# First token tile of a mixture-of-experts sum: weighted on TensorE by diagonal products, with the order of the tile's steps changed

## The chip, the cores and the metric

One core of a Trainium2 chip runs the whole program. The metric is device time in microseconds (us), the median of several executions.

## What is computed

Two transformer blocks for 512 tokens of width 1024. The first has differential attention, a state-space branch and a mixture of 32 experts, of which each token takes four; the second has a recurrent branch and dilated attention. The change lies where the first block ends and the second begins:

```python
y_rows = y_rows * row_gate[:, None]
y = jnp.zeros((n_tok, d)).at[row_tok].add(y_rows)     # four expert rows per token, each with its gate
x = x + g2[:, None, :] * y
x = _rmsnorm(x, final_g)
h = rms_norm(x, g_norm) * (1.0 + scale[:, None, :]) + shift[:, None, :]
q, k, v, ... = split(h @ w_in)
```

## The kernel before

The experts have written their output rows to `y_rows` in memory, one row per token and choice. The 512 tokens are four tiles (0 to 3) of 128. After the last expert the four tiles pass through the same steps, tile after tile, each engine in the fixed order in which its program is written; semaphores are all that joins the engines.

- **GpSimd** (`gpsimd_engine`, L2467) issues 16 indirect gathers, four per tile: 128 rows of 1024 floats each into `parts`. Tile 0's four have a semaphore each ("first parts k gathered"), the other tiles one for all four.
- **VectorE** (`vector_engine`): `add_part(t, k)` (L2168, L2170) multiplies a tile's gathered rows by their gates and adds them up, in four instructions of 128x1024. `residual(t)` (L2181, eight of 128x128, in two halves of four) adds the turned sum times `g2` to `x_t`. `tile_scale(t)` (L2187) is one reciprocal; `tile_scaled(t)` (L2193, eight of 128x128) makes `h_t` from `x_t`.
- **TensorE** (`tensor_engine`): `second_bias(t)` (L1037) puts the gated output bias in the two banks of tile t's sum. `turn_sum(t)` (L1045) transposes the sum of VectorE onto it, eight products of 128 columns with the identity. `norm_sums(t)` (L1053) makes sums over the squares, eight products of 2 columns. `spread_scale(t)` (L1059) puts the scale on all partitions. `v_rows(t, i)` (L1071) is the first real work of block two: half i of the value projection, eight products of 512 columns. `keep_on(count, bank)` (L610) issues `count` products of 512 columns whose result nobody reads ("idle products" below).
- **ScalarE** (`scalar_engine`): `tile_squares(t)` (L1519, two halves), `tile_root(t)` (L1523), `tile_shifted(t)` (L1528, eight pieces, each releasing one product of `v_rows`), `keep_v_rows(t, i)` (L1532). After tile 0's shift it issues the load of two tables (positions and the recurrent gates).
- **SyncE** loads the second half of the value weights once tile 0's fourth gather has landed, and waits for all gathers before it goes on to the weight pairs (L1112 are their products).

Every fp32 product is two passes on TensorE, so eight products are 16 records in the trace. The order on TensorE from the bias of tiles 0 to 2 on is: 6 idle products, `turn_sum(0)`, 2 idle, `norm_sums(0)`, 2 idle, `spread_scale(0)`, `turn_sum(1)`, `v_rows(0, 0)`, `norm_sums(1)`, `v_rows(0, 1)`, `spread_scale(1)`, `turn_sum(2)`, `v_rows(1, 0)`, and so on.

Of the kernel before, what the change touches and what calls it, by code (L numbers as in the profile page):

```python
# [14 lines left out]
P = 128  # L15
S = 512
D = 1024
KT = D // P
# [7 lines left out]
EXPERTS, TOPK = 32, 4  # L26
# [16 lines left out]
NP = len(PASSES)  # L43
# [74 lines left out]
def program(nc, io):  # L118


    with ExitStack() as ctx:
# [3 lines left out]
        def sem(name):  # L125
            if name not in sems:
                sems[name] = ctx.enter_context(nc.semaphore(name.replace(" ", "_")))
            return sems[name]
# [31 lines left out]
        psum = ctx.enter_context(nc.psum_tensor("psum", [P, 8, S], F32))  # L160
# [134 lines left out]
        pos_i = pos_i.bitcast(I32)  # L295
        parts = arena[:, 0:16 * D].rearrange("p (n d) -> p n d", n=16)
        g2 = mods[:, 40:48]
        rstd, rstd2 = work[:, 8, :], work[:, 8, :]
# [237 lines left out]
        def tensor_engine():  # L536
# [494 lines left out]
            def second_bias(t):  # L1031
# [7 lines left out]
                mm.then_inc(sem("bias in banks"), 1)  # L1039

            def turn_sum(t):
                a = SUM_AT[t]
                pe.wait_ge(sem("parts summed"), t + 1)
                for k in range(KT):
                    mm = pe.matmul(psum[:, a + k // 4, (k % 4) * P:(k % 4 + 1) * P], parts[:, t * TOPK, k * P:(k + 1) * P], identity, start=False, stop=True, skip_group_check=True)  # L1045
                    if k % 4 == 3:
                        mm.then_inc(sem("sum turned"), 1)
# [15 lines left out]

            def v_rows(t, i):
                if t == 0:
                    pe.wait_ge(sem(f"slot {4 + 4 * i} loaded"), 32 if i else V_LOADED)
                else:
                    pe.wait_ge(sem("v rows kept"), 2 * t + i - 1)
                for k in range(KT):
                    pe.wait_ge(sem("h ready"), 8 + KT * t + k + 1)  # L1070
                    mm = pe.matmul(psum[:, 4 + i, :], h_t[:, k, t * P:(t + 1) * P], ring[:, 4 * i + 4:4 * i + 8, k, :], start=(k == 0), stop=(k == KT - 1))  # L1071
                mm.then_inc(sem("v product"), 1)

# [5 lines left out]
            second_bias(2)  # L1079
            keep_on(6, 0)  # L1080
            turn_sum(0)
            keep_on(2, 0)
            norm_sums(0)
            keep_on(2, 0)
            spread_scale(0)
            turn_sum(1)
            v_rows(0, 0)
            norm_sums(1)
            v_rows(0, 1)
            spread_scale(1)  # L1090
# [149 lines left out]
        def scalar_engine():  # L1240
# [298 lines left out]
            act.dma_start(pos_i, io["positions"]).then_inc(sem("late tables loaded"), 16)  # L1539
            act.dma_start(arena[:, low:low + 2048], io["rnn_gates"]).then_inc(sem("late tables loaded"), 16)  # L1540
            tile_squares(1)
            keep_v_rows(0, 0)
            tile_root(1)
# [124 lines left out]
        def vector_engine():  # L1668
# [492 lines left out]
            def add_part(t, k):  # L2161
                acc = parts[:, t * TOPK, :]
                if t == 0:
                    dve.wait_ge(sem(f"first parts {k} gathered"), 16)
                elif k == 0:
                    dve.wait_ge(sem(f"parts {t} gathered"), 16 * TOPK)
# [22 lines left out]
            def tile_scaled(t):  # L2189
                dve.wait_ge(sem("scale spread"), t + 1)  # L2190
                dve.wait_ge(sem("moe added"), 2 * t + 2)
                for k in range(KT):
                    dve.scalar_tensor_tensor(h_t[:, k, t * P:(t + 1) * P], x_t[:, k, t * P:(t + 1) * P], gain2[:, k:k + 1], psum[:, 0, t * P:(t + 1) * P], ALU.mult, ALU.mult).then_inc(sem("h scaled"), 1)  # L2193

            for k in range(TOPK):
                add_part(0, k)
            residual(0)
            for k in range(3):
                add_part(1, k)
            tile_scale(0)  # L2200
            add_part(1, 3)
            tile_scaled(0)
            residual(1)
# [482 lines left out]
```

## Time and profile before

| | us |
|---|---|
| median of 3 runs | 1996.19 |
| lowest and highest | 1994.83, 1996.49 |
| the profiled execution, its own time | 1998.96 |
| its span, first to last instruction | 1997.7 |
| TensorE busy in the span | 1937.8 (97%) |
| VectorE busy | 836.2 (42%) |
| ScalarE busy | 424.7 (21%) |
| GpSimd busy | 240.0 (12%) |
| mean granted clock of TensorE | 0.987 |

Times in the trace count from the span's start. The stage of the change lies between 1340 and 1442 us. A granted clock of 1.00 is 2.4 GHz, one of 0.50 is 1.2 GHz. The difference between the profiled execution's own time and its span, 1.3 us, lies around the instructions.

### The profile page before, as it was taken

How to read it: one execution, taken by the hardware profiler on the slowest of the kernel's cores; microseconds unless marked ns; L12 is line 12 of the kernel's file. 1: busy time of each engine (PE TensorE's matmuls, PEld its weight loads, DVE VectorE, ACT ScalarE, POOL GpSimd, SP SyncE). 2: the span in 40 equal slices, each digit the busy share in tenths (PEclk: the TensorE clock that was granted, in tenths of full speed). 3: DMA queues.
4: the chain of work that ended last, by engine and by line, in shares of the span. 5: the costliest groups of instructions: out<-in, count | busy, mean ns of one | idle time of the engine just before them, and what ended most of it. 6: DMA issues, size and time to landing. Idle time of an engine off the chain costs nothing.

```text
span 1997.7 us, 38345 instructions
## 1 busy us (share of the span) xinstructions
PE 1937.8 (97%) x16481; PEld 1079.1 (54%) x16481; DVE 836.2 (42%) x1530; ACT 424.7 (21%) x914; POOL 240.0 (12%) x173
## 2 busy tenths in 40 slices
PE   8999998999999999999999999989999999999998
PEld 4455544433434434343443433345588888888887
DVE  5989875211121211121120211105458678654465
ACT  3223512210111110011010111102233443431102
POOL 0000000000000000000000000002244334360011
PEclk8999998999999999999999999998999999999999
DMA  8475796999799999999999999975112112122221
GB/s 339 139 282 195 286 335 268 420 419 366 319 421 419 420 420 419 421 419 420 419 419 420 418 420 416 419 295 225 63 68 89 67 67 89 66 85 85 85 85 64
DMA packets 103419, 553.94 MB, mean 277 GB/s; under 512 B 14224, under 2 KB 25488, under 8 KB 48336
## 3 DMA queue, kind: packets, MB, share of 16 engines
q1 hardware_dynamic: 81344, 516.84, 64.1%
q10 hardware_dynamic: 14848, 17.82, 2.7%
q0 software_dynamic: 7056, 16.79, 2.3%
q8 instruction: 133, 2.18, 0.4%
q14 instruction: 38, 0.31, 0.0%
HBM read 532.91 MB, written 26.35 MB: 280 GB/s over the span
## 4 chain that ended last, share of the span: by engine, by line
PE 72%; DMA 13%; SPq 10%; DVE 3%; issue 2%; ACT 1%; another core or an unknown queue 0%; ACTq 0%; DVEq 0%
PE psum L1112 24%; PE psum L926 19%; DMA arena<-in_w 9%; SPq L467 9%; PE psum L934 9%; PE psum L597 7%; PE psum L1071 3%; DMA ring<-in_w 2%; DMA arena<-in_mod_slabs 1%; PE psum L919 1%; PE psum L1199 1%; PE psum L1218 1%; PE psum L942 1%; PE psum L906 1%; PE psum L781 1%
## 5 line engine op out<-in xcount | busy, mean ns | idle before, releaser
L926 PE MATMUL psum<-arena,ring 128*32 128x512 f32 x4096 | 452.7, 596 | 11.3 <-DMA arena<-in_w 10.8
L926 PEld LDWEIGHTS psum<-arena,ring 128*32 128x32 f32 x4096 | 134.3, 110 | 310.1 <-issue 307.1
L2114 DVE TENSOR_SCALAR h_t<-psum 128x512 f32<-128x512 f32 (+2 forms) x33 | 27.9, 845 | 572.5 <-PE psum L926 572.5
L934 PE MATMUL psum<-arena,h_t 128*32 128x256 f32 x3840 | 217.9, 380 | 4.2 <-DMA arena<-in_w 3.3
L1458 ACT ACTIVATE ring<-psum,mods,gain 128x64 f32<-128x64 f32 (+2 forms) x264 | 85.6, 429 | 607.5 <-PE psum L906 607.5
L934 PEld LDWEIGHTS psum<-arena,h_t 128*32 128x32 f32 x3840 | 120.7, 110 | 101.1 <-issue 18.7
L2435 POOL DMA_INDIRECT ring<-h_rows,row_i x33 | 35.5, 1075 | 1144.0 <-PE psum L906 834.9
L1112 PE MATMUL psum<-ring 128*128 128x256 f32 x768 | 171.1, 379 | 0.0
L1112 PEld LDWEIGHTS psum<-ring 128*128 128x128 f32 x768 | 145.9, 190 | 20.1 <-issue 0.3
L1112 PE MATMUL psum<-h_t,ring 128*128 128x256 f32 x672 | 154.3, 379 | 0.2 <-ACT arena L1532 0.2
L926 PE MATMUL psum<-ring 128*32 128x512 f32 x1344 | 148.8, 593 | 5.5 <-DMA ring<-in_w 5.4
L1112 PEld LDWEIGHTS psum<-h_t,ring 128*128 128x128 f32 x672 | 126.4, 190 | 23.8 <-issue 7.7
L597 PE MATMUL psum<-h_t,ring 128*128 128x512 f32 x256 | 116.8, 611 | 2.5 <-ACT h_t L1278 2.5
L1112 PE MATMUL psum<-arena,ring 128*128 128x256 f32 x544 | 119.1, 379 | 0.0
L1112 PEld LDWEIGHTS psum<-arena,ring 128*128 128x128 f32 x544 | 103.3, 190 | 14.2 <-DVE arena L2268 0.2
L926 PEld LDWEIGHTS psum<-ring 128*32 128x32 f32 x1344 | 44.4, 110 | 103.4 <-issue 103.4
L934 PE MATMUL psum<-ring,h_t 128*32 128x256 f32 x1600 | 90.9, 380 | 3.8 <-DMA ring<-in_w 3.1
L2128 DVE COPY h_t<-psum 128x512 f32<-128x512 f32 (+2 forms) x33 | 27.9, 845 | 154.9 <-PE psum L942 154.9
L597 PEld LDWEIGHTS psum<-h_t,ring 128*128 128x128 f32 x256 | 48.7, 195 | 62.9 <-issue 61.8
L1466 ACT ACTIVATE work<-psum 128x512 f32<-128x512 f32 (+2 forms) x33 | 23.8, 720 | 240.8 <-PE psum L934 240.8
L934 PEld LDWEIGHTS psum<-ring,h_t 128*32 128x32 f32 x1600 | 50.2, 110 | 43.8 <-issue 7.8
L1112 PE MATMUL psum<-work,ring 128*128 128x256 f32 x256 | 60.7, 380 | 1.7 <-DVE work L2268 1.7
(480 smaller groups left out, 2132.6 us busy)
## 6 DMA issues: line engine op xcount, KB each, us to landing
arena<-in_w SPq DMA_DIRECT2D x288, 1024.0 KB, 30.9
ring<-in_w SPq DMA_DIRECT2D x96, 1024.0 KB
ring<-in_pairs SPq DMA_DIRECT2D x40, 1024.0 KB, 4.8
ring<-in_dot_slabs SPq DMA_DIRECT2D x40, 512.0 KB, 5.9
ring<-in_mod_slabs SPq DMA_DIRECT2D x6, 2048.0 KB, 9.2
ring<-in_proj_slabs SPq DMA_DIRECT2D x24, 512.0 KB, 4.4
y_rows<-arena SPq DMA_DIRECT2D x3, 3584.0 KB, 25.0
y_rows<-work ACTq DMA_DIRECT2D x70, 64.0 KB, 7.7
```

What stands on the lines that cost most here:

```text
L467: sp.dma_start(slot[s], source).then_inc(sem(f"weights {s} loaded"), 16)
L597: mm = pe.matmul(bank, ring[:, n % 4, k, :], src[:, k, :], start=(k == 0), stop=(k == KT - 1))
L781: mm = pe.matmul(bank, w_glu[:, m, k, :], proj[:, k, :], start=(k == 0), stop=(k == 3))
L926: mm = pe.matmul(psum[32 * j:32 * j + 32, g, :], x_e[:, c * tokens + g * TG:c * tokens + g * TG + TG], slot[s][:, j * S:(j + 1) * S], star ...
L934: mm = pe.matmul(psum[32 * j:32 * j + 32, 6 + g // 2, (g % 2) * 256:(g % 2) * 256 + 256], h_e[:, g * 256 + half * P + 32 * c:g * 256 + hal ...
L1071: mm = pe.matmul(psum[:, 4 + i, :], h_t[:, k, t * P:(t + 1) * P], ring[:, 4 * i + 4:4 * i + 8, k, :], start=(k == 0), stop=(k == KT - 1))
L1112: mm = pe.matmul(out, stationary[:, k, :], moving[:, k, :], start=(start and k == 0), stop=(k == 3), skip_group_check=True)
L1458: act.activation(x_e[:, k * tokens:(k + 1) * tokens], psum[:, 4 + k // 4, (k % 4) * tokens:(k % 4 + 1) * tokens], ACT.Identity, bias=mods[ ...
L1466: act.activation(dst[:, 0:256 * groups], src[:, 0:256 * groups], ACT.Copy).then_inc(sem("y kept"), 1)
L2114: dve.tensor_scalar(gate, psum[:, 0:groups, 0:256], LIMIT, None, ALU.min).then_inc(sem("gate clipped"), 1)
L2128: dve.tensor_copy(h_e[:, 0:256 * groups], src[:, 0:256 * groups]).then_inc(sem("h_e kept"), 1)
L2435: pool.indirect_dma_start(out=x_g[n][0:rows, :], out_offset=None, in_=h_rows, in_offset=bass.IndirectOffsetOnAxis(ap=index, axis=0), bound ...
```

## The change

Tile 0's weighted sum is no longer made on VectorE. VectorE makes four diagonal matrices (`by_gate`, the identity times one gate column each, 128x128), and TensorE multiplies each gathered part by its diagonal matrix, as soon as that part's semaphore allows, adding up in the same banks in which the bias lies (`turn_parts`). The transposition comes with it, so `turn_sum(0)` goes. The six idle products before it go too, and of the two behind `norm_sums(0)` one.

The order changes as well: `v_rows(0, 0)` now stands ahead of `turn_sum(1)`, and `norm_sums(1)` stands in the middle of `v_rows(0, 1)`. On VectorE all of tile 1's sum comes behind `tile_scaled(0)`. On ScalarE `keep_v_rows(0, 0)` comes ahead of `tile_squares(1)`.

```diff
--- before.py
+++ after.py
@@ -294,6 +294,7 @@
         halves = [tile(n)[0:ROT, :] for n in (7, 10)]
         pos_i = pos_i.bitcast(I32)
         parts = arena[:, 0:16 * D].rearrange("p (n d) -> p n d", n=16)
+        by_gate = x_g[1][:, 0:TOPK * P].rearrange("p (k n) -> p k n", k=TOPK)
         g2 = mods[:, 40:48]
         rstd, rstd2 = work[:, 8, :], work[:, 8, :]
         v_sb = arena[:, 0:4096].rearrange("p (h t n) -> p h t n", h=HEADS2, t=TT)
@@ -1038,9 +1039,19 @@
                                    start=(k % 4 == 0), stop=False, skip_group_check=True)
                 mm.then_inc(sem("bias in banks"), 1)
 
+            def turn_parts():
+                a = SUM_AT[0]
+                pe.wait_ge(sem("gates laid out"), TOPK)
+                for part in range(TOPK):
+                    pe.wait_ge(sem(f"first parts {part} gathered"), 16)
+                    for k in range(KT):
+                        mm = pe.matmul(psum[:, a + k // 4, (k % 4) * P:(k % 4 + 1) * P], parts[:, part, k * P:(k + 1) * P], by_gate[:, part, :], start=False, stop=(part == TOPK - 1), skip_group_check=True)
+                        if part == TOPK - 1 and k % 4 == 3:
+                            mm.then_inc(sem("sum turned"), 1)
+
             def turn_sum(t):
                 a = SUM_AT[t]
-                pe.wait_ge(sem("parts summed"), t + 1)
+                pe.wait_ge(sem("parts summed"), t)
                 for k in range(KT):
                     mm = pe.matmul(psum[:, a + k // 4, (k % 4) * P:(k % 4 + 1) * P], parts[:, t * TOPK, k * P:(k + 1) * P], identity, start=False, stop=True, skip_group_check=True)
                     if k % 4 == 3:
@@ -1061,7 +1072,7 @@
 
             V_LOADED = 16 * (1 + 2 * (ROWS_TO - 2) + 2 * (9 - ROWS_TO) + 1)
 
-            def v_rows(t, i):
+            def v_rows(t, i, between=None):
                 if t == 0:
                     pe.wait_ge(sem(f"slot {4 + 4 * i} loaded"), 32 if i else V_LOADED)
                 else:
@@ -1069,6 +1080,8 @@
                 for k in range(KT):
                     pe.wait_ge(sem("h ready"), 8 + KT * t + k + 1)
                     mm = pe.matmul(psum[:, 4 + i, :], h_t[:, k, t * P:(t + 1) * P], ring[:, 4 * i + 4:4 * i + 8, k, :], start=(k == 0), stop=(k == KT - 1))
+                    if between and k == 3:
+                        between()
                 mm.then_inc(sem("v product"), 1)
 
             pe.wait_ge(sem("b2 loaded"), 32)
@@ -1077,16 +1090,14 @@
             second_bias(0)
             second_bias(1)
             second_bias(2)
-            keep_on(6, 0)
-            turn_sum(0)
+            turn_parts()
             keep_on(2, 0)
             norm_sums(0)
-            keep_on(2, 0)
+            keep_on(1, 0)
             spread_scale(0)
+            v_rows(0, 0)
             turn_sum(1)
-            v_rows(0, 0)
-            norm_sums(1)
-            v_rows(0, 1)
+            v_rows(0, 1, lambda: norm_sums(1))
             spread_scale(1)
             turn_sum(2)
             v_rows(1, 0)
@@ -1538,8 +1549,8 @@
             act.sem_inc(sem("held"), 1)
             act.dma_start(pos_i, io["positions"]).then_inc(sem("late tables loaded"), 16)
             act.dma_start(arena[:, low:low + 2048], io["rnn_gates"]).then_inc(sem("late tables loaded"), 16)
+            keep_v_rows(0, 0)
             tile_squares(1)
-            keep_v_rows(0, 0)
             tile_root(1)
             keep_v_rows(0, 1)
             tile_shifted(1)
@@ -2160,9 +2171,7 @@
 
             def add_part(t, k):
                 acc = parts[:, t * TOPK, :]
-                if t == 0:
-                    dve.wait_ge(sem(f"first parts {k} gathered"), 16)
-                elif k == 0:
+                if k == 0:
                     dve.wait_ge(sem(f"parts {t} gathered"), 16 * TOPK)
                 if k == 0:
                     then(dve.tensor_scalar(acc, acc, gates[:, t, 0:1], None, ALU.mult))
@@ -2192,14 +2201,14 @@
                 for k in range(KT):
                     dve.scalar_tensor_tensor(h_t[:, k, t * P:(t + 1) * P], x_t[:, k, t * P:(t + 1) * P], gain2[:, k:k + 1], psum[:, 0, t * P:(t + 1) * P], ALU.mult, ALU.mult).then_inc(sem("h scaled"), 1)
 
+            dve.wait_ge(sem("x turned"), NP)
             for k in range(TOPK):
-                add_part(0, k)
+                dve.tensor_scalar(by_gate[:, k, :], identity, gates[:, 0, k:k + 1], None, ALU.mult).then_inc(sem("gates laid out"), 1)
             residual(0)
-            for k in range(3):
+            tile_scale(0)
+            tile_scaled(0)
+            for k in range(TOPK):
                 add_part(1, k)
-            tile_scale(0)
-            add_part(1, 3)
-            tile_scaled(0)
             residual(1)
             for k in range(TOPK):
                 add_part(2, k)
```

TensorE, from behind the bias products of tiles 0 to 2 to the first value products (L610 idle products, L1045 `turn_sum`, L1053 `norm_sums`, L1059 `spread_scale`, L1071 `v_rows`), before:

```order
L610 MATMUL psum<-consts 128x512 x6
L1045 MATMUL psum<-consts,arena 128x128 [waits parts_summed]
L1045 MATMUL psum<-consts,arena 128x128 x7
L610 MATMUL psum<-consts 128x512 x2
...
L610 MATMUL psum<-consts 128x512 x2
L1059 MATMUL psum<-consts,par 128x128 [waits tile_scale]
L1045 MATMUL psum<-consts,arena 128x128 [waits parts_summed]
L1045 MATMUL psum<-consts,arena 128x128 x7
L1071 MATMUL psum<-ring,h_t 128x512 [waits h_ready,slot_4_loaded]
L1071 MATMUL psum<-ring,h_t 128x512 [waits h_ready] x7
```

The same stretch in the changed kernel (L1048 `turn_parts`, L611 idle products, L1070 `spread_scale`, L1082 `v_rows`, L1056 `turn_sum`):

```order
L1048 MATMUL psum<-ring,arena 128x128 [waits first_parts_0_gathered,gates_laid_out]
L1048 MATMUL psum<-ring,arena 128x128 x7
...
L1048 MATMUL psum<-ring,arena 128x128 [waits first_parts_3_gathered]
L1048 MATMUL psum<-ring,arena 128x128 x7
L611 MATMUL psum<-consts 128x512 x2
...
L611 MATMUL psum<-consts 128x512
L1070 MATMUL psum<-consts,par 128x128 [waits tile_scale]
L1082 MATMUL psum<-ring,h_t 128x512 [waits h_ready,slot_4_loaded]
L1082 MATMUL psum<-ring,h_t 128x512 [waits h_ready] x7
L1056 MATMUL psum<-consts,arena 128x128 [waits parts_summed]
```

The products that carry tile 0's sum wait for the gathers themselves, and `v_rows(0, 0)` has moved ahead of tile 1's transposition.

VectorE in the changed kernel, from the end of the experts (L2206 the diagonal matrices, L2190 `residual`, L2196 `tile_scale`, L2202 `tile_scaled`, L2177 and L2179 `add_part`):

```order
L2206 TENSOR_SCALAR ring<-consts,cols 128x128 [waits x_turned]
L2206 TENSOR_SCALAR ring<-consts,cols 128x128 x3
L2190 SCALAR_TENSOR_TENSOR x_t<-psum,mods,x_t 128x128 [waits sum_turned]
...
L2196 RECIPROCAL par<-par 128x1 [waits tile_root]
L2202 SCALAR_TENSOR_TENSOR h_t<-x_t,par,psum 128x128 [waits moe_added,scale_spread]
L2202 SCALAR_TENSOR_TENSOR h_t<-x_t,par,psum 128x128 x7
L2177 TENSOR_SCALAR arena<-arena,cols 128x1024 [waits parts_1_gathered]
L2179 SCALAR_TENSOR_TENSOR arena<-arena,cols 128x1024 [waits dve_order] x3
```

Tile 1's first three `add_part` stood ahead of the reciprocal, and its fourth between the reciprocal and `tile_scaled(0)`; all four now follow `tile_scaled(0)`.

## Rows read from the trace of the kernel before

**Rows 1.** The page: the span.
```profile
span 1997.7 us, 38345 instructions
```

**Rows 2.** The chain of waits, 1330 to 1450 us: start, us, what.
```profile
1369.27 3.78 PE psum L1045 x16
1373.05 8.14 PE psum L1071 x16
1381.19 1.68 PE psum L1053 x16
...
1389.95 1.79 PE psum L1045 x16
1391.74 6.87 PE psum L1071 x16
```

**Rows 3.** Timeline of TensorE, 1335 to 1400 us: start, us, what.
```profile
1345.19 3.92 PE L1037 MATMUL psum<-work,ring 32*128 32x128 f32 x48
...
1355.88 2.05 PE L1045 MATMUL psum<-consts,arena 128*128 128x128 f32 x16 [1.42 <-issue]
1357.77 1.89 PE L610 MATMUL psum<-consts 128*128 128x512 f32 x4
...
1362.17 1.86 PE L1053 MATMUL psum<-par,h_t 128*128 128x2 f32 x8 [1.74 <-ACT h_t L1519]
1363.90 3.76 PE L610 MATMUL psum<-consts 128*128 128x512 f32 x4
1368.08 0.48 PE L1059 MATMUL psum<-consts,par 128*128 128x128 f32 x1 [0.42 <-DVE par L2187]
```

**Rows 4.** Timeline of VectorE, 1335 to 1400 us.
```profile
1348.99 0.82 DVE L2168 TENSOR_SCALAR arena<-arena,cols 128x1024 f32<-128x1024 f32 x1 [17.14 <-DMA arena<-y_rows,slot_i]
1351.67 2.60 DVE L2170 SCALAR_TENSOR_TENSOR arena<-arena,cols 128x1024 f32<-128x1024 f32 x2 [1.87 <-DMA arena<-y_rows,slot_i]
1354.54 1.28 DVE L2170 SCALAR_TENSOR_TENSOR arena<-arena,cols 128x1024 f32<-128x1024 f32 x1 [0.27 <-issue]
...
1360.33 1.13 DVE L2181 SCALAR_TENSOR_TENSOR x_t<-psum,mods,x_t 128x128 f32<-128x128 f32 x4 [1.75 <-remote]
1363.10 0.78 DVE L2168 TENSOR_SCALAR arena<-arena,cols 128x1024 f32<-128x1024 f32 x1 [1.64 <-DMA arena<-y_rows,slot_i]
...
1369.13 2.15 DVE L2193 SCALAR_TENSOR_TENSOR h_t<-x_t,par,psum 128x128 f32<-128x128 f32 x8
...
1374.13 0.75 DVE L2168 TENSOR_SCALAR arena<-arena,cols 128x1024 f32<-128x1024 f32 x1
...
1379.54 2.60 DVE L2170 SCALAR_TENSOR_TENSOR arena<-arena,cols 128x1024 f32<-128x1024 f32 x2
1383.27 0.16 DVE L2187 RECIPROCAL par<-par 128x1 f32<-128x1 f32 x1 [1.12 <-ACT par L1523]
```

**Rows 5.** Timeline of ScalarE, 1335 to 1400 us.
```profile
1361.49 0.63 ACT L1519 ACTIVATE h_t<-x_t 128x512 f32<-128x512 f32 x1 [2.25 <-issue]
...
1367.50 0.26 ACT L1523 ACTIVATE par<-psum,consts 128x1 f32<-128x1 f32 x1 [4.08 <-remote]
```

**Rows 6.** Windows: PE, PEld, DVE, ACT, POOL busy, granted clock, DMA share, GB/s.
```profile
308.00:311.40 3.40, 3.40 (x20) 3.21 (x19) 3.09 (x17) 1.42 (x3) 0.00 (x0) 0.63 1.01 426
...
1340.00:1345.00 5.00, 1.99 (x5) 0.60 (x4) 0.00 (x0) 0.00 (x0) 0.40 (x1) 1.00 0.26 80
...
1361.80:1365.20 3.40, 3.02 (x10) 2.51 (x11) 2.07 (x2) 1.61 (x2) 2.68 (x3) 0.50 1.03 420
1369.20:1375.50 6.30, 6.24 (x20) 4.69 (x21) 5.58 (x19) 3.71 (x10) 0.00 (x0) 0.50 1.04 414
1375.50:1382.70 7.20, 7.20 (x30) 4.09 (x29) 6.50 (x6) 0.60 (x1) 0.00 (x0) 1.00 0.24 97
```

**Rows 7.** The gathers of L2467, and SyncE's wait for the last of them.
```profile
L2467 POOL DMA_INDIRECT arena<-y_rows,slot_i x16: 933/938/1615, 1344.6 to 1364.4; - x16
...
L503 SPq EVENT_SEMAPHORE  x1: 17/17/17, 1376.0 to 1376.0; - x1
```

## The prediction

> **What bounds the kernel now.** I read the page first: the span is 1997.7 us [rows 1], and TensorE is busy for 97% of it, so a change counts only where TensorE idles, idles on purpose or runs at half clock. Next came the chain of waits over the stage of the change [rows 2]. From 1381.19 us on it is TensorE work without a gap: token sums 1.68, a half of the value rows 6.87, a transposed sum 1.79. Whatever brings the first product of `v_rows(1, 0)` (1391.74 us) forward brings the rest forward as well, because the weight pairs behind it are loaded on a count of value products, and I found nothing later that hangs on a fixed instant. So that start is my measure.
>
> Ahead of it the timelines of TensorE, VectorE and ScalarE [rows 3 to 5] show three things. First, tile 0's sum is serial: the fourth part is multiplied in at 1354.54, ends 1355.82, and only then are the turned products run, 1355.88 to 1357.93. Second, two releases come late. The second half of `residual(0)` starts at 1360.33, 2.4 us after the products it waits for, and `tile_root(0)` at 1367.50, 3.5 us after the end of the token sums (1362.17 + 1.86 = 1364.03). Both are put down to "remote", and behind both sets of products TensorE runs idle products. Third, the clock: 1.00 up to 1361.8, then 0.50 until 1375.5 [rows 6]. It fell after short 2-column products and gaps, and it came back when TensorE had been without a gap since 1369.27.
>
> **The sum of tile 0.** Removed from VectorE: 0.82 + 2.60 + 1.28 = 4.7 us [rows 4]. Added there: four 128x128 operations while VectorE idles (17.14 us of idle time ahead of the first part), so nothing. Added on TensorE: 4 x 8 products of 128 columns. Eight cost 2.05 us [rows 3] or 1.79 us [rows 2] at full clock; I take 1.95. The first group starts when the bias products end, 1345.19 + 3.92 = 1349.1, with its part there at 1348.99, and is done before the second part lands at 1351.67. The other parts land by 1354.54 at the latest, ahead of the groups that use them, so three groups run in a row: 1351.67 + 3 x 1.95 = 1357.5. Before it was 1357.9. The idle products that go stood in a wait and cost nothing there; what they covered was the clock, and that is the second rival. By itself this part gives 0.4 us.
>
> One rule bears on it. Two of the gathers' instructions took longer than the rest (maximum 1615 ns against a median of 938) [rows 7], and the page of the Trainium skill titled "SBUF — State Buffer", section "SBUF: two separate sides", says that VectorE in a two-port mode locks GpSimd out of writing descriptors. If the four sums were the cause, removing them would let the last gather be issued some 0.7 to 1.4 us earlier. I count nothing for it: the transfers themselves fill the DMA engines (share 1.03) [rows 6].
>
> **From the sum to the first value product.** Two late releases are the unknown term. Nothing in the trace tells their cause. Lower bound: they vanish. Upper bound: 2.4 us for the first (still two idle products behind it), and for the second the length of the one idle product left, half of 3.76 = 1.9 us at half clock [rows 3]. I take half of each, 1.2 and 0.9, being as far from one end as from the other. Then: release 1358.7; residual 1.13 [rows 4], 1359.8; squares 0.63 [rows 5], 1360.5; second half of the token sums 1.4, between the 1.86 shown at half clock [rows 3] and half of that at full clock, 1361.9; root at 1362.8, plus 0.26; reciprocal 0.16 and spreading 0.48, 1363.8; first slab of `tile_scaled` 2.15 / 8 = 0.3 [rows 4] and as much for its shift, 1364.4. There `v_rows(0, 0)` starts; before it stood behind the transposition of tile 1 and started at 1373.05. Its weights are loaded ahead of this stage, and before nothing waited for them.
>
> It takes 6.87 us plus half of the time at low clock. From 308 to 311.4 us the low clock ended within gapless products after some three quarters of the 3.4 us (mean 0.63) [rows 6], 2.5 us; here it lasted 6.2 us into them (1369.27 to 1375.5). I take 4.8 us, nearer to the row of this stage, so the half costs 9.3 us and ends at 1373.7.
>
> **The order behind it.** VectorE ends `tile_scaled(0)` 2.15 us after 1363.9, and then needs about 4.7 us for tile 1's sum, whose parts are there at 1363.10 [rows 4]: ready at 1370.8, ahead of need. So `turn_sum(1)` runs 1373.7 to 1375.5, and `residual(1)` is over at 1376.7. Now VectorE has seven `add_part` ahead of the reciprocal: 1374.13 to 1379.54 + 2.60 = 8.0 us [rows 4]. The gathers of tile 3 have all landed by 1376.0 [rows 7]; the table loads that ScalarE now issues earlier may push that to 1378, still ahead of their use at 1381.4. The reciprocal is at 1384.7, while TensorE comes to `spread_scale(1)` at 1375.5 + 6.87 + 1.68 = 1384.1. So **VectorE is late there, by 0.6 us**, a wait that was not there before: TensorE stands, with `turn_sum(2)` queued behind it. Then 0.16 + 0.3 + 1.79: `v_rows(1, 0)` starts at 1387.0, and its first slab is ready then (1.27 for the last `add_part`, 0.6 for the slab, 1386.8).
>
> The sum: 1391.7 - 1387.0 = **4.7 us less**. The move of `norm_sums(1)` into the middle of a half costs nothing in itself; it starts the squares' chain 3.4 us sooner, and without it the wait would be on ScalarE's root. Against the profiled execution, 1998.96 us, this is 1994.3. The median of the runs lies 2.8 us under that, and I apply the same difference there: 1996.19 - 4.7 = 1991.5 us. Its own two ends: with no late release and no low clock, `v_rows(0, 0)` starts at 1362.1, `turn_sum(1)` ends at 1370.9, VectorE at 1380.0 to 1381.3, the start is at 1383, 8.5 us less (1987.7); with both late in full it is the first rival.
>
> **Rivals.**
>
> *First: the releases stay late.* The start of `v_rows(0, 0)` moves from 1364.4 to 1366.9 (1.2 for the first release, 1.0 for the second, 0.5 for sums at half clock), and all behind it follows: 2.1 us less, 1994.1. For it: both late releases have idle products behind them, while `tile_root(1)`, behind whose sums real products run, comes at once (sums over at 1381.19 + 1.68 = 1382.87 [rows 2], reciprocal already at 1383.27 [rows 4]). Against it: the DMA engines were full at both late releases and idle at the prompt one, so the idle products need not be the cause.
>
> *Second, slower: the clock falls while TensorE waits for the parts.* Now nothing dense stands between 1349 and 1357, only groups of 128 columns with a gap of 0.6 us. If the clock falls by 1351.7, each group takes 3.78 us [rows 2] in place of 1.95: the parts' products end at 1363.0, not 1357.5. Residual and squares to 1366.0, idle products to 1366.8, token sums 2 x 1.86 to 1370.5, idle product to 1372.4, value products from 1373.5, their end 1382.8, `residual(1)` 1385.7, VectorE 1393.7, next start 1396.0: 4.3 us more, 2000.5. It decides from the second slow group on: with only the last group slow, the idle products end at 1363.1 and the sums at 1366.9, 5.0 us later than forecast, which just uses up the gain. Against it: the clock stayed at 1.00 from 1340 to 1345, with TensorE busy for only 1.99 of the 5 us [rows 6], and the 3.92 us of small bias products behind that [rows 3] did not bring it down. The page "TensorE: Matmul & The Clock Gate", section "HAM oscillation — how this bites in real kernels" of the Trainium skill, speaks for this rival: short bursts between waits for transfers put the engine back to its lower clock, and it then starts each burst slow.
>
> *Third: the low clock lasts as long as before.* If the clock returns only at 1375.5 although the value products have run since 1364.4, these take 11.1 us for 5.55 of their 6.87 and end at 1376.8, 3.1 us later than forecast: 1.6 us less, 1994.6. For it: the clock stayed low through products that were nearly gapless from 1369.2 to 1375.5 (6.24 of 6.30 us) [rows 6].
>
> **How the numbers follow.** 0.2% is 4.0 us, about what a measurement of this kernel can tell from no change. The forecast with its own spread has 0.66; 0.54 of that lies over 4.0 us of gain, 0.12 under. The first rival has 0.14, the third 0.10, both within 0.2%. The slower one has 0.10. That makes faster 0.54, the same 0.36, slower 0.10. The range has to leave out at most 0.2: it starts at the forecast's own lower end, 1987.5, takes in the first and the third rival, and ends at 1997.0, leaving out most of the slower case.
>
> **What the changed profile would show.** Four groups of sixteen 128-column records from 1349 to 1357.5, at about 1.95 us each; `v_rows(0, 0)` at 1364 rather than 1373, ahead of `turn_sum(1)`; the clock low for about 7 us, not 14; a short TensorE wait on VectorE's reciprocal ahead of `spread_scale(1)`; no "remote" longer than one idle product. I am wrong if the groups take 3.8 us, if VectorE is not the one waited for at `spread_scale(1)`, or if TensorE idles between 1387 and the end of the value rows, which would mean that something there is tied to an instant.

## The result, and the profile after

| | before | changed |
|---|---|---|
| median, us (20 runs each) | 1997.84 | 2002.96 |
| lowest, highest | 1991.22, 2002.67 | 1999.62, 2007.64 |
| profiled execution, its own time | 1998.96 | 2001.83 |

The ratio is 1.0025, 95% interval 1.0015 to 1.0034: slower, and outside the range of the prediction. The page's span, which answers to [rows 1]:

```profile
span 2000.5 us, 38410 instructions
```

The timeline of TensorE (start, us, what), to be held against [rows 3]:

```profile
1341.39 7.17 PE L1038 MATMUL psum<-work,ring 32*128 32x128 f32 x48
1348.50 6.06 PE L1048 MATMUL psum<-ring,arena 128*128 128x128 f32 x29
1354.81 0.51 PE L1048 MATMUL psum<-ring,arena 128*128 128x128 f32 x3 [0.25 <-issue]
1356.24 0.27 PE L1048 MATMUL psum<-ring,arena 128*128 128x128 f32 x1 [0.92 <-issue]
1357.65 0.79 PE L1048 MATMUL psum<-ring,arena 128*128 128x128 f32 x2 [1.14 <-issue]
1359.77 0.37 PE L1048 MATMUL psum<-ring,arena 128*128 128x128 f32 x1 [1.32 <-issue]
1360.48 0.58 PE L1048 MATMUL psum<-ring,arena 128*128 128x128 f32 x1 [0.34 <-issue]
1361.90 0.37 PE L1048 MATMUL psum<-ring,arena 128*128 128x128 f32 x1 [0.84 <-issue]
1363.30 5.08 PE L1048 MATMUL psum<-ring,arena 128*128 128x128 f32 x26 [1.03 <-issue]
...
1373.81 7.11 PE L1082 MATMUL psum<-ring,h_t 128*128 128x512 f32 x16 [0.97 <-ACT h_t L1539]
...
1392.19 0.32 PE L1070 MATMUL psum<-consts,par 128*128 128x128 f32 x1 [0.83 <-DVE par L2196]
...
1394.15 6.25 PE L1082 MATMUL psum<-ring,h_t 128*128 128x512 f32 x14
```

The 64 diagonal records take 19.9 us (1348.50 to 1368.4), where the forecast had 8.4. In the middle only nine records run from 1354.81 to 1363.30, with gaps between them put down to "issue": TensorE waits for nothing that the profile shows. The pieces start at 1354.81, 1356.24, 1357.65, 1359.77, 1360.48, 1361.90 and 1363.30, so they are 1.43, 1.41, 2.12, 0.71, 1.42 and 1.40 us apart: one, two or three times 0.70 us. I call this **the holds**. Each part is a group of 16 records, and all but one of the gaps (the one behind the 32nd record) fall inside a group, so it isn't a late part that is waited for.

The windows (columns as in [rows 6]) add the clock:

```profile
1344.00:1350.00 6.00, 6.00 (x42) 5.78 (x39) 0.00 (x0) 0.00 (x0) 4.47 (x6) 0.50 0.91 313
1350.00:1356.00 6.00, 5.07 (x27) 4.96 (x27) 0.00 (x0) 0.00 (x0) 4.47 (x6) 0.68 1.01 408
1356.00:1362.00 6.00, 2.11 (x6) 1.29 (x5) 0.00 (x0) 0.00 (x0) 3.40 (x4) 0.61 1.03 415
1362.00:1368.00 6.00, 4.97 (x26) 4.98 (x26) 0.66 (x3) 0.00 (x0) 0.00 (x0) 0.54 1.03 410
```

In slices of 1 us the granted clock is 0.50 through the bias products (7.17 us, not 3.92 as in [rows 3]) and the first records, 1.00 from 1354 to 1357, and 0.50 again from 1358 to 1367: it came back just as the holds began and fell again in the middle of them. At full clock 64 records took 8.14 us (y2 below), 0.127 us each. The first 29 took 6.06 us, 2.4 more than at that pace; the last 26 took 5.08, 1.8 more; the rest, 7.6 us, is the holds.

VectorE and the gathers, against [rows 4] and [rows 7]:

```profile
1367.34 2.19 DVE L2190 SCALAR_TENSOR_TENSOR x_t<-psum,mods,x_t 128x128 f32<-128x128 f32 x8 [35.69 <-PE psum L1048]
...
1389.33 2.60 DVE L2179 SCALAR_TENSOR_TENSOR arena<-arena,cols 128x1024 f32<-128x1024 f32 x2
1391.97 0.16 DVE L2196 RECIPROCAL par<-par 128x1 f32<-128x1 f32 x1
```

```profile
L2476 POOL DMA_INDIRECT arena<-y_rows,slot_i x16: 934/938/954, 1340.7 to 1359.4; - x16
```

No release is late any more: the residual starts as soon as the sum is there. The last of the sixteen gather instructions ends 19.6 us after the first began. The ones of 1615 ns are gone: none takes over 954 ns with no sum of VectorE beside them, and in y1 and y2 below, where tile 1's sum runs beside the held gathers, one takes 1.71 us. By the page "SBUF — State Buffer" of the Trainium skill, section "SBUF: two separate sides", VectorE in a two-port mode locks GpSimd out of writing descriptors. The trace agrees as far as it goes; which mode VectorE was in, no row shows. Where little else differs this gained no time, as forecast: all sixteen gathers had landed 31.6 us after the first began in r_before, which has the four sums, and 31.7 us in e4, which has not.

For all that follows, **the stage** is the time from the first gather's issue to the start of `v_rows(1, 0)`: 1344.6 to 1391.6 (the timeline's start), 47.0 us before, and 1340.7 to 1394.15, 53.5 us after. The prediction amounts to 42.4 (1387.0 less 1344.6). From `v_rows(1, 0)` to the end of the span it is 606.1 to 606.7 us in all twenty profiles of this study, and ahead of the first gather the change adds only VectorE's four small operations, so the stage must carry it. The first gather's own start scatters between 1336.7 and 1345.4, whichever kernel runs.

### The profile page after: what moved, and what is told of

Same layout as the page of the kernel before. It is cut to its first block, busy times and chain, and to the rows that moved or that the text cites. A ratio compares the mean times of both kernels' runs of the same rounds, so it can differ in the third digit from the quotient of the medians.

```text
span 2000.5 us, 38410 instructions
## 1 busy us (share of the span) xinstructions
PE 1935.8 (97%) x16515; PEld 1082.8 (54%) x16515; DVE 831.0 (42%) x1530; ACT 425.2 (21%) x914; POOL 238.3 (12%) x173
## 4 chain that ended last, share of the span: by engine, by line
PE 68%; DMA 15%; SPq 11%; DVE 4%; issue 2%; ACT 1%; DVEq 0%; POOLq 0%; ACTq 0%
PE psum L1123 24%; PE psum L927 18%; SPq L468 10%; DMA arena<-in_w 9%; PE psum L935 7%; PE psum L598 6%; DMA ring<-in_w 3%; PE psum L1082 2%; DMA arena<-in_mod_slabs 1%; PE psum L1210 1%; PE psum L1229 1%; PE psum L920 1%; DMA h_rows<-ring 1%; PE psum L1048 1%; PE psum L782 1%
```

## The experiments

Eighteen runs on four chips, B to E; which chip gave the first result isn't known. The chips differ by as much as the change does, so each ratio is taken against the kernel before on the same chip. (r2_before is that kernel against itself: 1.0008 is what no change at all can show.) "Holds" says whether the profile shows them, and until how long after the first gather.

| run | chip | ratio, 95% | stage, us | holds |
|---|---|---|---|---|
| e1_load_last | B | 1.0032, 1.0021 to 1.0043 | 48.7 | no |
| e2_before_load_last | B | 1.0020, 1.0010 to 1.0029 | 46.5 | no |
| e3_order_only | B | 1.0000, 0.9990 to 1.0010 | 40.3 | no |
| e4_diagonal_only | B | 1.0003, 0.9991 to 1.0015 | 43.5 | no |
| r_before | B | one run, not timed | 44.6 | no |
| r_after | B | 0.9993, 0.9982 to 1.0005 | 40.5 | no |
| e5_order_no_wait | B | 0.9994, 0.9981 to 1.0007 | 42.5 | no |
| e6_idle_between | B | 1.0004, 0.9992 to 1.0017 | 44.8 | no |
| r2_before | C | 1.0008, 0.9994 to 1.0022 | 49.4 | late release, 22.7 |
| r2_after | C | 1.0035, 1.0020 to 1.0050 | 50.7 | 22.3 |
| e7_no_wait | C | 1.0031, 1.0018 to 1.0044 | 51.0 | 22.6 |
| e8_before_no_six | C | 1.0008, 0.9993 to 1.0022 | 43.5 | late release, 22.4 |
| x1_load_behind_tile1 | D | 1.0021, 1.0010 to 1.0032 | 56.9 | 22.6 |
| x2_load_first | D | 1.0023, 1.0010 to 1.0036 | 52.6 | 22.8 |
| x3_after | D | 1.0016, 1.0005 to 1.0026 | 57.0 | 22.7 |
| x4_order_only | D | 1.0004, 0.9990 to 1.0019 | 51.1 | late release, 22.5 |
| y1_hold_gathers | E | 0.9995, 0.9984 to 1.0006 | 40.6 | no |
| y2_no_wait_hold | E | 0.9990, 0.9975 to 1.0005 | 37.4 | no |

The median of the kernel before was 1990 to 1991 us on chip B, 1995.6 on C, 1997.9 on D, 1991.5 on E, and 1997.8 in the first result. Holds or late releases show where it is slow: on C, on D and in the first result. A stage is one execution's, a ratio that of many; within one kernel the stage moves by several us with the clock, so the ratios decide. On chip C, for one, the medians are 7 us apart (r2_after 2002.47, the kernel before 1995.56), while the two profiled stages differ by 1.3 us.

### Is it the load of the value weights?

SyncE issues the load of the second half of the value weights once the fourth part has landed, and its transfer runs beside the holds. First theory: that load triggers them.

```diff
 # SyncE, e1_load_last (changed kernel) and e2_before_load_last (before)
             sp.wait_ge(sem("first parts 3 gathered"), 16)
-            load_v(1)
             for k in range(1, TT):
                 sp.wait_ge(sem(f"parts {k} gathered"), 16 * TOPK)
+            load_v(1)
```

> The changed kernel with one edit: SyncE issues the second half of the value weights only when all 16 gathers have landed, not after tile 0's fourth. In the changed kernel TensorE crept from 1354.56 to 1363.30 us of its trace, ten records of the diagonal products in 8.7 us, and in just that time (1354.3 to 1364) the load of these weights shared the DMA engines with the gathers. Theory L (the load beside the gathers is what slows TensorE): the creep is gone, the diagonal products are over some 8 us sooner, about 1356 to 1360 by the clock they get, and the time is 4 to 8 us under the changed kernel, so a ratio of 0.998 to 1.0005 to the kernel before. Theory G (the gathers alone do it, some 14 us after the first): the creep stays where it is, the ratio stays near 1.0025. Theory C (only the low clock matters): the creep stays or the groups take 3.8 us each, ratio 1.001 to 1.003.

> The kernel before with the same edit. Theory L: its two late releases (2.4 us behind the turned sum, 3.5 us behind the token sums), which lie inside the time of that load (1356.9 to 1367.5), are gone; the time falls by up to 3 us, because tile 1's gathers then bound VectorE, and they come sooner too without the load beside them; ratio 0.998 to 1.000. Theory G or a fault of the idle products: the late releases stay, ratio 1.000. If the value weights come too late for v_rows(0, 1), TensorE waits there and the ratio is 1.001.

TensorE's timeline of e1_load_last:

```profile
1342.38 2.02 PE L1048 MATMUL psum<-ring,arena 128*128 128x128 f32 x16 [0.64 <-DMA arena<-y_rows,slot_i]
1344.91 5.62 PE L1048 MATMUL psum<-ring,arena 128*128 128x128 f32 x48 [0.51 <-DMA arena<-y_rows,slot_i]
...
1373.04 6.37 PE L1082 MATMUL psum<-ring,h_t 128*128 128x512 f32 x8 [8.16 <-DMA ring<-in_v_slabs]
```

The diagonal records ran as the prediction had them, and the late load was waited for, 8.16 us (3.54 in the kernel before), so that the ratio missed what was expected. That looked like proof until the unchanged kernels ran on the same chip.

> The kernel before, unchanged, for its profile on this chip. The four runs so far showed no late release and no creep, though in two of them the load of the value weights shared the DMA engines with the gathers at full share. Theory E (late releases and creep are an episode of single executions or of the first chip, and no part of the kernel): here both releases of tile 0 come within 0.5 us, and from the first gather to the first product of v_rows(1, 0) some 41 us pass, not 47. Theory L in its first form has fallen if so.

> The changed kernel, unchanged, beside the kernel before on this chip. Theory E with theory C (what the change costs in earnest is that the bias and diagonal products run at half clock once the idle products are gone, and VectorE's wait at spread_scale(1)): no creep, ratio 1.000 to 1.001. If the creep belongs to the changed kernel: it shows again between 14 and 23 us after the first gather, and the ratio is 1.0025 again.

```profile
1341.68 4.12 PE L1038 MATMUL psum<-work,ring 32*128 32x128 f32 x48
1345.90 8.71 PE L1048 MATMUL psum<-ring,arena 128*128 128x128 f32 x64
...
1360.05 7.11 PE L1082 MATMUL psum<-ring,h_t 128*128 128x512 f32 x16 [0.96 <-ACT h_t L1539]
...
1380.03 0.32 PE L1070 MATMUL psum<-consts,par 128*128 128x128 f32 x1 [2.44 <-DVE par L2196]
```

Chip B has no holds with the load where it was, so e1 and e2 said nothing of their cause; they show only what a late load costs. (r_before has no late release, as expected, but a stage of 44.6 us for some 41: more on that under the idle products.) On a chip with holds (D) the load was moved both ways:

```diff
 # SyncE, x1_load_behind_tile1
             sp.wait_ge(sem("first parts 3 gathered"), 16)
+            sp.wait_ge(sem("parts 1 gathered"), 16 * TOPK)
             load_v(1)
-            for k in range(1, TT):
+            for k in range(2, TT):
 # SyncE, x2_load_first
-            sp.wait_ge(sem("first parts 3 gathered"), 16)
             load_v(1)
+            sp.wait_ge(sem("first parts 3 gathered"), 16)
```

> The changed kernel with SyncE's load of the second half of the value weights issued when tile 1's gathers have landed, some 6 to 9 us later than now. Theory L (the load beside the gathers triggers the creep), on a chip with the creep: the diagonal products run through without a gap and end 8 to 9 us sooner after the first gather; the load then falls under v_rows(0, 0), whose long products bear it; ratio to the kernel before 0.998 to 1.000 where the changed kernel is 1.003. Theory G (something else at 14 to 23 us after the first gather): the gaps stay, ratio 1.002 to 1.0035. On a chip without the creep: like the changed kernel, or up to 1 us slower if the weights come too late.

> The changed kernel with that load issued ahead of the gathers, as soon as its slots are free. Theory L: the load is over by the time the third and fourth group run, and no gap is left in them; tile 0's first parts land up to 5 us later, since 2 MB more stand before them, so the groups end 4 us or so sooner than in the creeping kernel, ratio 1.000 to 1.002. If the creep follows the load to its new place, gaps show in the first groups instead. Theory G: gaps at the same distance from the first gather as before.

> The changed kernel once more, for the ratio on this chip: 1.0025 to 1.0035 with the creep in its profile, or 0.999 to 1.000 without it.

SyncE's timeline of x1, and TensorE's around its first holds:

```profile
1358.35 0.41 SPq L473 DMA_DIRECT2D ring<-in_v_slabs  x1
```

```profile
1352.17 4.85 PE L1049 MATMUL psum<-ring,arena 128*128 128x128 f32 x21
1357.27 0.68 PE L1049 MATMUL psum<-ring,arena 128*128 128x128 f32 x3 [0.25 <-issue]
1359.40 0.27 PE L1049 MATMUL psum<-ring,arena 128*128 128x128 f32 x1 [1.46 <-issue]
...
1365.76 6.82 PE L1049 MATMUL psum<-ring,arena 128*128 128x128 f32 x35 [1.03 <-issue]
```

The first two gaps begin at 1357.02 and 1357.95, both ahead of the load. In x2 the load came first:

```profile
1342.79 0.41 SPq L473 DMA_DIRECT2D ring<-in_v_slabs  x1
```

```profile
1352.49 7.73 PE L1048 MATMUL psum<-ring,arena 128*128 128x128 f32 x46 [4.35 <-DMA arena<-y_rows,slot_i]
1362.14 0.39 PE L1048 MATMUL psum<-ring,arena 128*128 128x128 f32 x2 [1.92 <-issue]
...
1366.40 3.15 PE L1048 MATMUL psum<-ring,arena 128*128 128x128 f32 x14 [0.36 <-issue]
```

The first part came 4.35 us late, so the records ran later; the holds ended at 1366.40, 22.8 us after the first gather (1343.60), as in the others. **The load is not the cause: this theory fell.** (x3, the changed kernel as it was, had the holds and a ratio of 1.0016, less than the 1.0025 to 1.0035 expected with them.) What stays put is the instant after the first gather: with diagonal products the holds end at 22.3 to 22.8 us and begin at 12.6 to 14 (in x2, whose records start late, at 16.6).

### Which part of the change meets the holds?

e3_order_only and x4_order_only keep VectorE's sum, `turn_sum(0)` and the six idle products and take over the rest of the change; e4_diagonal_only takes the diagonal products and leaves the order as before.

> The kernel before with the change's order alone: v_rows(0, 0) ahead of turn_sum(1), norm_sums(1) in the middle of v_rows(0, 1), one idle product behind the first token sums, tile 1's sum on VectorE behind tile_scaled(0). Tile 0's sum stays on VectorE with its six idle products. By the forecast's own sum the order is worth most of the gain: 3 to 5 us, ratio 0.9975 to 0.9985. Against it: VectorE's seven part sums between residual(1) and the reciprocal of tile 1 let TensorE wait at spread_scale(1), which could eat it: ratio 1.000.

> The changed kernel with the old order behind tile 0's sum: diagonal products alone. Theory L: 64 records of TensorE run into the load, the creep of 8 to 9 us stays, and this is the kernel that carries the whole loss: ratio 1.004 to 1.006, above the changed kernel's 1.0025. If the order carries the loss: ratio 0.999 to 1.000.

> Order alone once more (tile 0's sum on VectorE, six idle products). On a chip with the creep, if the diagonal products are what the creep hits: 0.999 to 1.0005, with late releases of 2 to 3 us as in the kernel before. If the order is hit as well (its chain of tile 0 is one idle product shorter): 1.002 to 1.003.

> The kernel before against itself, to see what the comparison makes of no change, and for one more profile of it. Expected ratio 1.000, interval some 0.001 to either side. If this job falls on a chip of the first kind (the kernel before at 1998 rather than 1990 us), its profile shows late releases in tile 0's stage again; on a chip of the second kind it does not.

> The changed kernel again. Theory E: on a chip on which the kernel before takes 1990 us the ratio is 0.999 to 1.0 and no creep shows; on one on which it takes 1998 us the creep shows between 14 and 23 us after the first gather, and the ratio is 1.002 to 1.003. If the creep is a matter of single executions, it shows or not without regard to the chip.

On chip B neither half can be told from no change. On chip D the order alone is level too (1.0004), where the whole change is slower (1.0016). Its VectorE shows where the same instants go when no diagonal products lie there:

```profile
1359.39 1.13 DVE L2182 SCALAR_TENSOR_TENSOR x_t<-psum,mods,x_t 128x128 f32<-128x128 f32 x4 [5.64 <-remote]
1364.37 1.13 DVE L2182 SCALAR_TENSOR_TENSOR x_t<-psum,mods,x_t 128x128 f32<-128x128 f32 x4 [3.85 <-remote]
```

These are the late releases of [rows 4], longer here, and the kernel before has one in r2_before as well:

```profile
1368.11 1.13 DVE L2181 SCALAR_TENSOR_TENSOR x_t<-psum,mods,x_t 128x128 f32<-128x128 f32 x4 [2.46 <-remote]
```

The last wait that the holds delay ends 22.4 to 22.9 us after the first gather (in the kernel before as first profiled: root at 1367.50, 22.9). So late releases and holds are, by their time and by the chips on which they appear, most likely one thing: TensorE is held, and what is in flight there (a semaphore's update in the one kernel, the next record in the other) comes when it lets go. The kernel before meets it with the releases of two sets of products, the changed one with the middle of its 64 records. That the diagonal products are the part that costs on such a chip rests on comparing x4 with x3, whose intervals overlap; e4 wasn't tried there.

### The six idle products and the clock

```diff
 # e8_before_no_six: before
-            keep_on(6, 0)
             turn_sum(0)
 # e6_idle_between: the changed kernel's turn_parts, behind each part, and ahead of it
+                    keep_on((1, 0, 0, 0)[part], 0)
...
+            keep_on(2, 0)
             turn_parts()
```

> The kernel before without its six idle products ahead of turn_sum(0), nothing else changed; TensorE then idles some 6 to 12 us while VectorE sums tile 0. Theory C (the six products buy the clock): the granted clock is 0.50 when turn_sum(0) begins and stays there through tile 0's chain, some 10 us of products at half speed, 2 to 5 us more, ratio 1.001 to 1.0025. If they buy nothing: 1.000.

> The changed kernel with two idle products ahead of the first group of diagonal products and one behind it, where TensorE would wait for gathers at full clock. Theory C: the granted clock is back at 1.00 before the groups or in their first ones, the groups take 1.9 to 2.2 us each, and the time falls by 1 to 4 us against the changed kernel on the same chip. If the clock does not matter: 0 to 2.7 us slower, the length of the idle products.

TensorE's timeline of e8:

```profile
1345.38 3.92 PE L1037 MATMUL psum<-work,ring 32*128 32x128 f32 x48
1354.86 3.78 PE L1045 MATMUL psum<-consts,arena 128*128 128x128 f32 x16 [5.55 <-issue]
```

Without the six, TensorE stood for 5.55 us and `turn_sum(0)` ran at half clock, 3.78 us for 1.95; the price is 1.0008, which is also what the kernel before showed against itself. In r_before the other case is seen: the bias products at half clock (7.17 us), then twelve dense idle records in 8.03 us, the clock back at 1.00 from 1353 on, and the turned sum behind them at full clock, 1.95. But there the idle products were not free. VectorE's sum was over at 1349.6, and `turn_sum(0)` stood behind them until 1355.42, 5.8 us; in r2_before it stood 5.0 us, and in the first profile of the kernel before, with its bias products at full clock, 0.1. So the six buy the clock at a price that depends on the clock they start at, which may be why taking them out moved nothing. In e4, with the same slow bias products and no six, the diagonal records took 9.59 us. Idle records put back between the parts (e6) brought the groups to full clock (1.95 us for the first, 5.52 for the other three) and yet gained nothing that can be measured on chip B: 1.0004 beside 0.9993 of r_after, intervals overlapping.

### The wait on VectorE

```diff
 # VectorE, e7_no_wait (and with the order alone: e5_order_no_wait)
-            for k in range(3):
-                add_part(3, k)
             tile_scale(1)
-            add_part(3, 3)
             tile_scaled(1)
             residual(2)
+            for k in range(TOPK):
+                add_part(3, k)
```

> Order alone, with VectorE's four add_part of tile 3 moved behind residual(2), so that only tile 2's four stand ahead of the reciprocal of tile 1. In order alone TensorE waited 1.99 us there (with 1.07 us of that for a gather). If that wait is what ate the order's gain: it is gone from the trace and the time is 2 us lower, ratio 0.9985 to 0.9995. If not: 1.000.

> The changed kernel with tile 3's four add_part behind residual(2) on VectorE. In its last profile TensorE waited 2.44 us for VectorE's reciprocal ahead of spread_scale(1), 1.5 us of it for tile 3's gathers. With only tile 2's sum ahead of the reciprocal the wait goes, and v_rows(1, 0) starts 2 to 2.4 us sooner after the first gather: ratio 0.998 to 0.999. If another wait takes its place (TensorE at second_bias(3) or turn_sum(3)), the ratio stays at the changed kernel's.

In both the wait ahead of `spread_scale(1)` is gone, and neither ratio moves beyond its interval (0.9994 beside 1.0000 of e3; 1.0031 beside 1.0035 of r2_after, where 0.998 to 0.999 was expected). e5's `v_rows(0, 0)` took 10.16 us at a low clock, e7 had its holds: both are larger than the wait.

### Fewer gathers in a row

```diff
 # GpSimd, y1_hold_gathers (changed kernel) and y2_no_wait_hold (e7_no_wait)
             for n in range(TT * TOPK):
+                if n == 2 * TOPK:
+                    pool.wait_ge(sem("sum turned"), 2)
                 pool.indirect_dma_start(
```

> The changed kernel, but GpSimd issues the eight gathers of tiles 2 and 3 only when tile 0's sum is turned (all of it). Theory G (TensorE is held in steps of about 0.7 us from some 13 us after the first gather to some 3 us after the end of the sixteenth, because gathers pile up behind full DMA engines): with eight gathers the holds stay away or end by 3 us after the eighth, about 13 us after the first gather, so the 64 diagonal records run at an even pace; the stretch from the first gather to the first product of v_rows(1, 0), 53.5, 50.7 and 57.0 us in the changed kernel on chips with holds, is 43 to 47 there. The holds may come back 13 us after the first gather of the second eight, then in the value products. Rival T (the holds hang on the time since the experts' end or since the first gather alone, whatever GpSimd issues): held from 13 to 22.6 us after the first gather as before, stretch 50 to 57, ratio 1.002 to 1.0035. On a chip without holds both theories say the same: 0.9995 to 1.002, because tile 3's parts land some 6 us later than before and VectorE, which adds them ahead of tile 1's reciprocal, may make TensorE wait up to 5 us there.

> The same hold of the gathers of tiles 2 and 3, and tile 3's four add_part stand behind residual(2), so that nothing of tile 3 stands ahead of tile 1's reciprocal. Theory G on a chip with holds: even diagonal records, no wait at spread_scale(1) (under 0.5 us), stretch 41 to 45 us, ratio 0.998 to 1.000, the best of the kernels with diagonal products there. Rival T: stretch about 51, ratio 1.003 as in the run without the hold. On a chip without holds: stretch 40 to 42.5, ratio 0.999 to 1.0. Tile 2's parts land by 31 us after the first gather, tile 2's sum is wanted later than that.

Both fell on a chip without holds, so **what triggers them stays open**. One candidate falls to the traces on hand: in six changed kernels with holds (after, r2_after, e7, x1 to x3) the last packet that loads instructions starts 3.6 to 6.2 us after the first gather, and the next, where the trace shows one, not before 37 us, so no load of instructions runs beside the holds. TensorE's timeline of y2:

```profile
1343.80 8.14 PE L1048 MATMUL psum<-ring,arena 128*128 128x128 f32 x64
...
1357.38 7.11 PE L1082 MATMUL psum<-ring,h_t 128*128 128x512 f32 x16 [0.96 <-ACT h_t L1539]
...
1374.76 0.27 PE L1070 MATMUL psum<-consts,par 128*128 128x128 f32 x1
...
1376.66 7.03 PE L1082 MATMUL psum<-ring,h_t 128*128 128x512 f32 x16
```

This is the stage with full clock, even records and no wait: 37.4 us, the shortest seen. Yet over twelve runs the ratio is 0.9990 with an interval that holds 1, so it isn't shown to beat the kernel before either, and on a chip with holds it wasn't run.

## Why the prediction was wrong

- **The step that failed** is the one on the sum of tile 0: "three groups run in a row: 1351.67 + 3 x 1.95 = 1357.5". Its records, 8.14 us at full clock, took 19.9: 7.6 of holds and 4.2 of half clock, 1.8 of these behind the holds, in the middle of which the clock had fallen again. They also began 3.3 us later than forecast, counted from the first gather (7.8 for 4.5), because the bias products ran at half clock, 7.17 us for 3.92. So the sum was over 27.7 us after the first gather, and not 12.9. From there to `v_rows(0, 0)` it was 5.4 us for 6.9, with no late release left; `v_rows(0, 0)` was forecast at 19.8 us and came at 33.1.
- **Behind it, the unknown that was halved.** The two late releases were taken as delays that belong to idle products, to be halved or lost. In the runs their end lies at a nearly fixed distance, some 22.7 us, from the first gather. The change did not remove what made them late; most likely it put its own products into that time. The row for it was there: the residual's second half and the root came 15.7 and 22.9 us after the first gather, and TensorE's 16 turned records carry an idle time "issue" of 1.42 us in [rows 3]. I priced the delay of a release and not that of the records that would stand there.
- **The second rival** (slower; 2000.5) had the right sign and part of the mechanism: groups at half clock. It had the clock fall behind 1349, while TensorE waits for parts; in fact the clock was low from the bias products on, and a wait for parts (0.64 and 0.51 us in e1) did not bring it down. The half clock of the bias products isn't the change's doing: r_before and r2_before have it too (7.17 us). That this execution drew it was bad luck; half clock up to the holds explains 5.7 us (3.3 and 2.4), the holds and the slow records behind them the rest.
- **The third rival** did not happen: `v_rows(0, 0)` ran in 7.11 us, 2.2 less than the forecast's 9.3, the clock being back before it (in other profiles it took up to 10.16 us, e5). 13.3 later at its start and 2.2 given back make the 11.1 us by which the stage missed (53.5 against 42.4).
- **The wait on VectorE** was forecast at 0.6 us and measured 0.83, 2.44 on chip B, where VectorE itself waited 1.52 us for tile 3's gathers, which the prediction had landed in time: right in place, small in price.
- **"Nothing later hangs on a fixed instant"** held: 606.1 to 606.7 us everywhere.
- **The idle products that "stood in a wait and cost nothing"** were so in the first profile; in r_before and r2_before they outlasted the wait by 5.8 and 5.0 us. Over many runs taking them out shows no price either way (e8, 1.0008).
- **On the chips without holds** the working was nearer: stage 40.5 us in r_after for 42.4 forecast, 4.1 less than r_before for 4.7. That closeness is luck: r_before had no late releases to lose, and 5.8 us of its stage are idle products that ran past the sum. The ratio over many runs, 0.9993, is 1.4 us, within the interval of no change. Over the twelve runs of r_after, times and mean granted clock go together (correlation -0.94; 1986.1 us at 0.993, 1995.15 at 0.988): one profile of each kernel compares two draws of the clock as much as two kernels.

## What to carry to other kernels

When two releases are late for no cause that the trace names, find the instant to which they are tied (here, by its distance, the first gather or what ends just ahead of it) before moving more small products into that stretch; what delays one semaphore may delay the records that take its place. Work that was serial on VectorE costs little on TensorE only if TensorE has its clock there and is not held. And where a few microseconds decide, run both kernels on more than one chip: the same change was 0.9993 on one and 1.0035 on another.

## What the runs showed of the hardware

- On chips C and D and in the first result TensorE was held in steps of 0.70 us, from some 13 until some 22.5 us after the first of sixteen indirect gathers, about 3 us after the last of them ended its issue in the changed kernel; in eight profiles on chip B and two on chip E never, with the DMA engines as full. No record, no queue's packet and no semaphore in the trace names a cause. It doesn't depend on the load of the value weights. Whether it takes many gathers, or only the time, is open, and so is why chips differ; whether recording the trace has a part in it, no run tests.
- A wait on TensorE's sum put down to "remote", with the records on time, is most likely how the holds look when few records stand in them (2.46 us in r2_before, 5.64 and 3.85 in x4).
- Without holds, 64 records of 128 columns ran in 8.14 us at full clock (y2), and in 8.71 (r_after), 9.59 (e4) and 10.16 us (y1) where the granted clock was 0.50 for a part of them. Twelve idle records of 512 columns, begun at 0.50, saw the clock back at 1.00 within their 8.03 us (r_before).
